# Decoder trunk step on one core: decode scores on 128 partitions, two weight units split after the attention loop, branch merges on VectorE

## The reference, cut to what matters

```python
for bi in range(N_BRANCH):       # (window, dilation) = (128,1), (512,4), (2048,16)
    o, lse = dilated_branch(q[:, :, bi], k_ext[bi], v_ext[bi], ...)
    # s = q.k * scale - slope_h * distance; o = softmax(s) @ v; lse = max + log(sum)
wts = softmax(stack(lses), axis=0)
out = sum(wts[..., None] * stack(outs), axis=0)
x = x + out.reshape(N, L, OUT_W_B) @ w_o
x = x + sq_relu_mlp(rmsnorm(x, norm_mlp[l]), w_up[l], w_down[l])
```

## Time and profile before

| | us |
|---|---|
| median of 3 runs | 2870.25 |
| the profiled execution, its own time | 2877.71 |
| its span in the profile | 2875.8 |
| TensorE busy | 2798.5 (97%) |
| VectorE busy | 1625.6 (57%) |
| ScalarE busy | 859.4 (30%) |
| GpSimd busy | 71.9 (3%) |
| mean granted TensorE clock | 0.981 of full |

### The profile page before, as it was taken

The page is one execution under the profiler, slowest core; times in us unless marked ns, Lnnn a source line. Parts: engine busy times, 40 slices in busy tenths (PEclk is TensorE's granted clock), DMA queues, the critical chain, the costliest instruction groups (busy, mean ns, idle before and its releaser), DMA issues.

```text
span 2875.8 us, 44523 instructions
## 1 busy us (share of the span) xinstructions
PE 2798.5 (97%) x18468; PEld 2729.1 (95%) x18468; DVE 1625.6 (57%) x2980; ACT 859.4 (30%) x1923; POOL 71.9 (3%) x94
## 2 busy tenths in 40 slices
PE   7999999999999999999999999997999999999998
PEld 7999999999869999999999999995799999999997
DVE  7777767776446544444544554557764544445445
ACT  6444434544214211112111322334441221112211
POOL 0000000000040000000000000001310000000000
PEclk9999999999799999999999999998999999999999
DMA  4010001102322111111111133323401111111101
GB/s 149 34 39 24 24 30 39 39 17 97 154 81 64 45 56 48 45 44 45 45 57 45 65 106 103 101 79 125 130 16 44 59 44 45 45 45 53 51 30 60
DMA packets 81415, 174.19 MB, mean 61 GB/s; under 512 B 21369, under 2 KB 46241, under 8 KB 80628
## 3 DMA queue, kind: packets, MB, share of 16 engines
q1 hardware_dynamic: 73300, 162.83, 16.7%
q10 hardware_dynamic: 7920, 8.56, 1.0%
HBM read 140.39 MB, written 36.21 MB: 61 GB/s over the span
## 4 chain that ended last, share of the span: by engine, by line
PE 91%; DVE 5%; ACT 1%; POOL 1%; issue 1%; DMA 1%; ACTq 0%; SPq 0%; DVEq 0%; POOLq 0%
PE psum L2023 18%; PE psum L2024 18%; PE psum L2025 18%; PE psum L2286 6%; PE psum L2097 4%; PE psum L2099 3%; PE psum L2098 3%; PE psum L2049 3%; PE psum L2530 2%; PE psum L2508 2%; PE psum L2466 1%; PE psum L2467 1%; PE psum L2468 1%; PE psum L2352 1%; PE psum L2277 1%
## 5 line engine op out<-in xcount | busy, mean ns | idle before, releaser
L2023 PE MATMUL psum<-x_hi,w_hi 128*128 128x352 f32 (+1 forms) x1040 | 334.8, 322 | 0.0
L2024 PE MATMUL psum<-x_lo,w_hi 128*128 128x352 f32 (+1 forms) x1040 | 332.7, 320 | 0.0
L2025 PE MATMUL psum<-x_hi,w_lo 128*128 128x352 f32 (+1 forms) x1040 | 331.1, 318 | 0.0
L1090 DVE SCALAR_TENSOR_TENSOR w_lo<-w_raw,gains,w_hi 128x512 fp32r<-128x512 f32 x380 | 264.7, 754 | 55.2 <-ACT w_hi L581 55.0
L581 ACT ACTIVATE w_hi<-w_raw,gains 128x512 fp32r<-128x512 f32 x380 | 246.9, 712 | 131.7 <-DMA w_raw<-in_w 125.3
L2097 PE MATMUL psum<-x_hi,w_hi 128*128 128x352 f32 (+1 forms) x768 | 272.3, 355 | 1.2 <-DVE pre L1172 1.2
L2023 PE MATMUL psum<-u_hi_b,w_hi 128*128 128x352 f32 (+1 forms) x768 | 246.8, 321 | 0.0
L2023 PE MATMUL psum<-x_hi_b,w_hi 128*128 128x352 f32 (+1 forms) x768 | 246.6, 321 | 0.0
L2023 PE MATMUL psum<-u_hi,w_hi 128*128 128x352 f32 (+1 forms) x768 | 246.5, 321 | 0.0
L2098 PE MATMUL psum<-x_lo,w_hi 128*128 128x352 f32 (+1 forms) x768 | 246.3, 321 | 0.0
L2099 PE MATMUL psum<-x_hi,w_lo 128*128 128x352 f32 (+1 forms) x768 | 246.2, 321 | 0.0
(11 more groups left out here) (354 smaller groups left out, 6058.5 us busy)
## 6 DMA issues: line engine op xcount, KB each, us to landing
w_raw<-in_w SPq DMA_DIRECT2D x190, 512.0 KB, 3.6
q_tile<-scratch_q SPq DMA_DIRECT2D x24, 256.0 KB, 2.9
scratch_att<-o_out ACTq DMA_DIRECT2D x32, 132.0 KB, 2.5
x<-in_x SPq DMA_DIRECT2D x8, 516.0 KB, 9.1
x_half<-in_x SPq DMA_DIRECT2D x2, 2064.0 KB, 22.7
s_state<-in_s_rec_in SPq DMA_DIRECT2D x2, 2048.0 KB, 13.9
out_s_rec<-s_state SPq DMA_DIRECT2D x8, 512.0 KB, 2.6
merge<-scratch_att SPq DMA_DIRECT2D x8, 512.0 KB, 3.6
```

What stands on the lines that cost most here:

```text
L1090: done = v.scalar_tensor_tensor(w_lo[:, slot, 2 * part + k], w_raw[:, part, k], gains[:, unit * UW + 2 * part + k:unit * UW + 2 * part + k ...
L2023: mm(out, whi, xh[:, k, cols], start=k == 0, stop=False)
L2024: mm(out, whi, xl[:, k, cols], start=False, stop=False)
L2025: done = mm(out, wlo, xh[:, k, cols], start=False, stop=k == kts - 1)
```

## The change

Five edits:

1. **Decode scores on 128 partitions.** The scores of sample n go to partitions 32*(n mod 4) and up, by a position in the array (`tile_position`), all into one bank. `s_p` becomes 128x422 in place of 8x1688; `s_qz` is padded from 8 to 32 columns per sample. Maximum and sum are taken per row (the sum by the exponential itself), and VectorE and ScalarE do what GpSimd did. Scores are made after the second turn of step 16, exponentiated and scaled in step 17, turned in step 18 (4 transposes in place of 16), applied in step 19.
2. **Merges by VectorE.** GpSimd's ten instructions per chunk go. VectorE makes the differences at the end of a step (`chunk_maxima`), the sums with one reduction (`weights`), and the two products and their sum (`merge_output`).
3. **Units 12 and 13 split after the loop.** Unit 12 is still loaded in steps 15 and 16, unit 13 after the loop; their four half-unit splits leave steps 17 to 20 and go between the last `add_output`s of VectorE, and into ScalarE's end of stage.
4. **More filling at the first place.** `dense_done` gives place 0 twelve triples in place of five, and the next 17 places 88 in place of 91.
5. **The samples' own values are loaded in step 17** in place of step 15.

```diff
-          12: ((10, 2, 0),), ..., 15: ((11, 3, 1),), 17: ((12, 0, 0),), 18: ((12, 0, 1),), 19: ((13, 1, 0),), 20: ((13, 1, 1),)}
+          12: ((10, 2, 0),), ..., 15: ((11, 3, 1),)}
 # dense_done
     if place < 18:
-        return max(96 * (place + 1) // 18, 0)
+        return 8 + 88 * (place + 1) // 18 if place >= 0 else 0
 # SP, attention_traffic
-                if step == 15:
+                if step == 17:
                     sp.wait_ge(sem("s_vnew_stored"), L.value("s_vnew_stored"))
...
+            for part in range(2):
+                weight(U_KVQ + 13, part)
 # ACT, stage_end and attention_layer
+                    if third == 0 and between == "attention" and k in (3, 6):
+                        split_hi(U_KVQ + 13, 1, (k // 6,))
...
-                if step == 18:
-                    act.wait_ge(sem("s_scores_ready"), L.next("s_scores_ready"))
-                    act.activation(s_p[:], s_p[:], ACT.Exp).then_inc(sem("s_exp_ready"), L.add("s_exp_ready"))
+                if step == 17:
+                    act.wait_ge(sem("s_maxima_ready"), L.next("s_maxima_ready"))
+                    for m in range(2):
+                        act.activation(s_p[:, m], s_p[:, m], ACT.Exp, bias=s_pm[:, 0, m:m + 1], accum_out=s_pm[:, 1, m:m + 1]
...
+            split_hi(U_KVQ + 12, 0)
             merge_high(CH - 1)
 # POOL: samples_scores, samples_shares and the loop over chunks are gone
-            pool.tensor_tensor(heads(part[:, 0]), heads(merge[:, par, 0]), by_head(share[:, 3, 1]), ALU.mult
...
 # DVE
+            def weights(c):
+                sums, own = merge_stats[:, c % 2, :, 1], stats[:, (16 + c) % 3, 1]
+                v.wait_ge(sem("probs_ready"), L.next("probs_ready", 8 if c else 8 * 17))
+                v.wait_ge(sem("shares_ready"), L.next("shares_ready"))
+                v.tensor_tensor(share[:, 2, 0], share[:, 1, 0], own, ALU.mult)...
+                v.tensor_tensor(share[:, 2, 1:3], share[:, 1, 1:3], sums, ALU.mult)...
+                v.tensor_reduce(total[:, 3], share[:, 2].rearrange("p b s -> p s b"), AXX, ALU.add)...
 # merge_output
+                for n in range(2):
+                    v.tensor_tensor(part[:, n], merge[:, c % 2, n], b3(share[:, 3, 1 + n], 8, HD), ALU.mult)...
+                v.tensor_tensor(part[:, 0], part[:, 0], part[:, 1], ALU.add)...
 # after the loop
                 add_output(n)
+                if n in (10, 11):
+                    split_lo(U_KVQ + 12, 0, (n - 10,))
+                if n in (14, 17):
+                    split_lo(U_KVQ + 13, 1, (n // 17,))
 # PE
+            def samples_scores():
+                for n in range(NS):
+                    rows, lo = slice(n % 4 * 32, n % 4 * 32 + 32), n // 4 * 256
+                    for b, first, last in ((0, 0, SA), (1, SA, SA + 65), (2, SA + 65, SA + 82), (0, SA + 82, SK)):
+                        done = mm(psum[rows, 1, lo + first:lo + last], s_qz[:, b, n], s_keys[:, n, first:last],
+                                  start=True, stop=True, tile_position=(0, n % 4 * 32))
```

More of the change, by code:

```diff
@@ L1858, in merge_output @@
                 v.wait_ge(sem("weights_ready"), L.value("weights_ready"))
+                for n in range(2):
+                    mark = "merge_free" if n else "dve_order"
+                    v.tensor_tensor(part[:, n].rearrange("p (n d) -> p n d", d=HD),
+                                    merge[:, c % 2, n].rearrange("p (n d) -> p n d", d=HD), b3(share[:, 3, 1 + n], 8, HD), ALU.mult
+                    ).then_inc(sem(mark), L.add(mark))
+                v.wait_ge(sem("dve_order"), L.value("dve_order"))
+                v.wait_ge(sem("merge_free"), L.value("merge_free"))
+                v.tensor_tensor(part[:, 0], part[:, 0], part[:, 1], ALU.add).then_inc(sem("dve_order"), L.add("dve_order"))
                 v.wait_ge(sem("bank7_full"), L.next("bank7_full"))
@@ L1878, in samples_queries @@
                     for b in range(BRANCH):
-                        v.tensor_copy(s_qz[rows, b].rearrange("p n (j g) -> p j g n", g=2)[:, :, g],
+                        v.tensor_copy(s_qz[rows, b, :, 0:8].rearrange("p n (j g) -> p j g n", g=2)[:, :, g],
                                       s_q[rows, 4 * b:4 * b + 4]).then_inc(sem("s_keys_ready"), L.add("s_keys_ready"))
@@ L1954, in attention_layer @@
                 if 18 <= step < 26:
-                    weights()
+                    weights(step - 18)
                 drain(3 * step)
@@ L1964, in attention_layer @@
                 drain(3 * step + 1)
-                if step == 16:
-                    samples_biased(0)
                 if prev and prev[0]:
@@ L1978, in attention_layer @@
                 if step == 16:
-                    samples_biased(1)
+                    samples_maxima()
                 if step == 17:
-                    samples_maxima()
-                if step == 18:
-                    samples_sums()
-                if step == 20:
+                    samples_shares()
+                if step == 19:
                     samples_outputs()
@@ L2543, in samples_rows @@
                 done.then_inc(sem("s_vrow_full"), L.add("s_vrow_full"))
-            def samples_scores(half):
-                if half == 0:
-                    pe.wait_ge(sem("s_keys_ready"), L.next("s_keys_ready", 9))
-                for n in range(4 * half, 4 * half + 4):
-                    m, lo = n // 2 % 2, (n % 2) * 256
-                    if n % 2 == 0:
-                        pe.wait_ge(sem(f"bank{1 + m}_free"), L.next(f"bank{1 + m}_free"))
+            def samples_scores():
+                pe.wait_ge(sem("s_keys_ready"), L.next("s_keys_ready", 9))
+                pe.wait_ge(sem("bank1_free"), L.next("bank1_free"))
+                for n in range(NS):
+                    rows, lo = slice(n % 4 * 32, n % 4 * 32 + 32), n // 4 * 256
                     for b, first, last in ((0, 0, SA), (1, SA, SA + 65), (2, SA + 65, SA + 82), (0, SA + 82, SK)):
-                        done = mm(psum[0:8, 1 + m, lo + first:lo + last], s_qz[:, b, n], s_keys[:, n, first:last],
-                                  start=True, stop=True)
-                    if n % 2:
-                        done.then_inc(sem(f"bank{1 + m}_full"), L.add(f"bank{1 + m}_full"))
+                        done = mm(psum[rows, 1, lo + first:lo + last], s_qz[:, b, n], s_keys[:, n, first:last],
+                                  start=True, stop=True, tile_position=(0, n % 4 * 32))
+                done.then_inc(sem("bank1_full"), L.add("bank1_full"))
             def samples_turn():
@@ L2560, in samples_turn @@
                 for bank, first, last in ((1, 0, SA), (2, SA, SK)):
-                    for n in range(NS):
-                        done = nc.tensor.transpose(psum[0:last - first, bank, 8 * n:8 * n + 8], s_p[:, n, first:last],
-                                                   ident[0:8, 0:8])
+                    for m in range(2):
+                        done = nc.tensor.transpose(psum[0:last - first, bank, m * P:(m + 1) * P], s_p[:, m, first:last], ident[:])
                 done.then_inc(sem("s_turned_full"), L.add("s_turned_full"))
@@ L2588, in attention_layer @@
                     fill(3 * step)
-                if step == 16:
-                    samples_scores(0)
+                if step == 18:
+                    samples_turn()
                 if step == 19:
-                    samples_turn()
-                if step == 20:
                     samples_apply()
```

120 lines of the change are left out of this document (44 added, 76 removed), and 2 rows, old and new, of the table SPLITS.

## The result

The changed kernel takes 2885.39 us (median of 5 runs, 2882.75 to 2890.13), the kernel before 2870.59 us (5 runs, 2868.25 to 2872.59). The ratio is 1.0049, 95% interval 1.0035 to 1.0064: **slower** by 0.5%, where 0.5% less was forecast. The profiled execution took 2890.13 us with a span of 2888.3, so 12.5 us more span than the one before.

A forecast was written before the change was run, and what follows sets the result against it. TensorE, busy 2798.5 of 2875.8 us, was taken as the bound, so only its idle or low-clock stretches pay. Terms -4.7 + 0.6 - 0.5 - 4.2 - 8.1 + 4.5 - 1.1 = -13.5 gave 2857 us, range 2846 to 2867.

The forecast's parts named there:

- Item 5: Steps 19 to 24: T1 to T0 4.6 us, T0 to T1 7.8; -8.1 in all, clock +4.5, bounds 0 and +13.
- the ring: A step's cycle in steps 19 to 24: T1, TensorE's apply and transposes, T0, VectorE's list, T1; 12.4 us forecast.
- B: Rival: pauses before applies keep TensorE at 1.2 GHz through steps 19 to 24; +12, 2882 us; chance 0.07.
- Item 1: Loop head: twelve triples ahead of the first scores fill TensorE's 4.04 us wait and spare the scores the low clock; -4.7.
- 2: Step 14: clearing `s_qz`, four times as wide, takes VectorE 0.8 us instead of 0.22; +0.6.
- Item 3: Steps 16 and 17: shorter sample rows without GpSimd save 2 us, three `s_vb` loads take back 1.5; -0.5.
- Item 4: Tail of step 17 and step 18: statistics' landing to end of T1 takes 11.8 us instead of 16.0; -4.2.
- Item 6: After the loop: four half-unit splits, 5.3 to 5.7 us, fit VectorE's 6.1 us of waits for TensorE; 0.
- The -1.1 for the last apply: Last apply of the loop: expected at 3.76 us instead of 4.85.
- A: Rival: VectorE's products by a broadcast share cost 1.04 us each, 8.4 us more; 2865 us; chance 0.13.
- D: Rival: TensorE's next stage waits for the splits after the loop; +5.3, 2862 us; chance 0.05.
- C: Rival, larger gain: no apply starts low, and samples' scores run side by side on four column groups; 2851 us; chance 0.13.

The follow-up runs named there:

- the version with T1 first: The changed kernel with the merge's two products with loaded outputs and two additions moved behind the copy T1: 2857.3 us, ratio 0.9955.

## Why the prediction was wrong

**Which step failed.** Item 5: "From T1 to T0 TensorE needs 3.76 + 0.88 = 4.6 us; this doesn't change", with 1.5 us, three times, for the clock. By starts of the copies (T1's own 0.6 counted behind T1), the forecast was 7.2 us from T0 to T1 and 5.2 from T1 to T0. VectorE's part was right, 7.3 us. TensorE's was not: in the six steps T1 to T0 sums to 51.1 us, 8.5 each, where 31 + 4.5 were forecast, and this 15 us is the error of the item. With three unread matmuls in the pauses the 51.1 become 43.6, and T0 to T1 falls from 45.8 to 42.9. In steps 19, 21 and 22 there T1 to T0 is 5.5 us, so 5.2 was a fair figure for full clock, and the clock was the term of the wrong size. 4.5 us were taken; in the changed kernel the applies of steps 18, 20, 21 and 23 take 2.9, 2.5, 1.5 and 1.7 us more than 3.76, and the transposes behind the first three, which the term didn't count, 0.8 to 0.9 each: 11.1 us. The unread matmuls gave back 10.4. What is left of the 43.6 over 31 lies in step 20 (9.6 us), which TensorE reaches late because step 19 holds the samples' apply (2012.91 to 2016.87 in the changed kernel, 3.96 us), which I had left out, and in steps 23 and 24 (7.0 and 10.6 us), which had output products but no extra matmuls.

The gain of 8.1 us at full clock rested on a second thing that is only half right, that the ring of before was long for VectorE's sake. In steps 19 to 21 it was: T0 waits for nobody there. In steps 22 to 24 T0 waited 3.0, 3.3 and 4.4 us for TensorE already. So the six steps add up like this: T0 to T1 went from 33.3 us to 45.8 (5.3 to 7.3 in steps 20 and 21), T1 to T0 from 51.8 to 51.1. VectorE's added work came in whole, and on the other half of the ring, where the gain was to be, the lowered clock took the place of VectorE's old waits.

**The rival that came true is B**, at 0.07. Its mechanism (the pause ahead of each apply) and its steps are as written; its price of 30 us was for every step at 1.2 GHz, and the applies measured 6.6, 3.7, 6.2, 5.3, 3.7, 5.5 and 4.7 us, so about half of it. That B's time, 2882, is so near the measured 2885 is in part luck: its six steps came some 10 us too dear, and the rest, where it kept the forecast's gains, about as much too cheap. The argument against B was that the pauses would be half of the 5.9 us one. The evidence against that stood in the trace of before, where pauses a quarter as long had already lowered the clock:

```profile
2048.14 4.62 PE L2530 MATMUL psum<-v_keys,prob_t 128*128 128x64 f32 x32 [1.59 <-DVE prob_t L1827]
2089.35 4.85 PE L2530 MATMUL psum<-v_keys,prob_t 128*128 128x64 f32 x32 [1.41 <-issue]
```

The prediction used the second, but called it the one "after a shorter stretch of work" and didn't look at the pause ahead of it. Behind half the planned pause an apply already cost 0.9 to 1.1 us more, and the transposes behind the first of them took 1.91 us in place of 1.04. The Trainium skill's section on HAM oscillation ("TensorE: Matmul & The Clock Gate"), which the prediction had set aside, describes this case: by it, bursts of matmuls between waits pay again and again for a clock that was lowered in the wait. The traces now agree: 6.63, 6.23 and 5.26 us behind waits of 3.1 to 3.4 us. They go further: behind waits of 1.1 us the clock was lowered in 9 of 15 applies (the table in the last section).

**Point by point.** Item 1 (-4.7) and 2 (+0.6): together -4.1 forecast, -4.0 measured at T1(15). The twelve scores took 3.2 us against 4.4. Alone, the filling gave 4.5 and the samples' part cost 1.4. Item 3 (-0.5): T1(17) came 3.9 us later, because TensorE waits 3.57 us for the query tile, which half of the samples' scores had hidden; the experiment that moves them gives 4.1 us back. The moved step was the cover of a transfer, and the prediction had not asked what it covered. Item 4 (-4.2): from the landing of the statistics to the end of T1(18) it is 12.0 us, before 16.1, so this item is right. With item 3 the forecast was -4.7, and T1(17) to T1(18) gave -2.8, because the statistics land later: 3.16 us after VectorE asks for them, behind three loads that take 2.08 us of SP's queue, where 1.5 was estimated:

```profile
1983.61 2.08 SPq L510 DMA_DIRECT2D s_vb<-scratch_s_vnew  x3
1985.80 0.59 SPq L454 DMA_DIRECT2D merge<-scratch_att  x1
1986.44 0.61 SPq L456 DMA_DIRECT2D merge_stats<-scratch_att  x1
```

```profile
1989.69 0.17 DVE L1800 TENSOR_TENSOR total<-merge_stats 128x8 f32<-128x8 f32 x1 [3.16 <-DMA merge_stats<-scratch_att]
```

Item 6 (0): T1(24) to the second MLP is 3.1 us longer. Of these, 1.9 to 2.0 are the splits. From the last transposes of `merged` to the second MLP's first product it is 25.4 us in all five profiles with the splits in the loop and 27.3 to 27.4 in all eight with the splits behind it, at granted clock 1.00 throughout, and only the eight have this wait of TensorE for VectorE (here the changed kernel's):

```profile
2130.09 0.79 PE L2035 MATMUL psum<-ones,sq_sums 128*88 128x1 f32 x8 [0.97 <-DVE sq_sums L1065]
```

The other 1.2 us lie ahead of these transposes. The -1.1 for the last apply didn't come either: it takes 4.72 us, before 4.85, behind a pause of 1.75. Of the rivals, A (dear products) is refuted by 1.28 us for two. D (the splits show) happened at over a third of its price, 1.9 us of 5.3. Of C, the side by side scores didn't happen: see the last section.

## What to carry to other kernels

When work moves to the engine that closes a ring (copy, apply, transpose, copy), put ahead of the copy only what frees a buffer for the waiting engine, and the rest behind it; here that alone was worth 27 us. A pause of TensorE costs itself and then, here always from 2.3 us on and often from 1 us on, the clock of what comes behind it. So read the length of a known instruction behind each pause of the trace, and pair the two before you price a pause that you plan. And a step that moves takes its cover along: ask which transfer it hid at its old place.

## What the runs showed of the hardware

Matmuls that nobody reads, in a pause, made the kernel faster: 3 per step took 2.7 us and gave back 2.9, 2.5 and 1.5 us in the applies of steps 18, 20 and 21 and about 0.8 us in the transposes behind each.

How a pause and the clock go together here can be counted over the seven applies of 32 matmuls, steps 18 to 24, in each of the thirteen profiles. An apply takes 3.7 to 3.8 us at granted clock 1.00 throughout, and longer where the clock falls to 0.5 in it:

| pause right before the apply, us | applies | of these 3.7 to 3.8 us | the others, us |
|---|---|---|---|
| under 0.1 | 43 | 43 | |
| 0.3 to 0.8 | 6 | 5 | 4.6 |
| 1.0 to 1.2 | 15 | 6 | 4.7 to 5.4 |
| 1.2 to 1.8 | 14 | 3 | 4.6 to 6.2 |
| 2.3 to 7.1 | 13 | 0 | 5.3 to 7.1 |

So at 1.1 us the length of the pause alone doesn't decide; what else does is not shown here. The versions with GpSimd's merges or with T1 first are faster than the changed kernel both by shorter pauses and by a clock that is lowered less often.

The samples' scores are 64 matmuls (as recorded) that go to four column groups of the array; the eight records of one sample go to one group, the next sample's to the next. Where the clock is 1.00 throughout, a sample takes 0.36 us (from 1971.07 us on in the version with T1 first), and with all samples on one group, before, 0.43 to 0.44 (from 1974.88 us on); the 3.96 us of the changed kernel hold three samples at a lowered clock. Four groups side by side would make it about a quarter of 0.43 (an estimate), so samples didn't run side by side in this order; where the 0.07 us come from is not shown. The Trainium skill ("TensorEngine Tiling (Array Packing)", section "Key Properties") says that different tiles can work in parallel; no run here shows it, and an order that changes the group from one matmul to the next wasn't tried.
